# One decoder step on one core: the forget gate's chain at unit 9, its softplus at unit 7, and decode scores at unit 16

## What is computed

```python
h = h + 0.5 * post1(SwiGLU1(pre1(h)))            # 1024 -> 2816 -> 1024
P = preM(h) @ w_in                               # one combined input projection
y = [A | B | C | D](P)                           # four mixers, 256 wide each
h = h + postM(y @ w_out)
h = h + 0.5 * post2(SwiGLU2(pre2(h)))
```

```python
log_a = log_sigmoid(a_lr @ w_a2 + b_a) / 16      # B: the GLA gate
logf  = log_sigmoid(pd[..., 768:772] + b_f)      # D: the forget gate, 4 heads
s     = q k^T / 8 + cumsum(logf)_q - cumsum(logf)_k   # D: prompt scores
```

## Time and profile before

| | before |
|---|---|
| median of 3 runs | 1093.97 us (1093.46 to 1093.98) |
| the profiled execution | 1094.53 us |
| its span, first to last instruction | 1092.7 us |
| mean granted TensorE clock | 0.993 |
| busy, share of the span | PE 97%, DVE 65%, ACT 50%, POOL 25% |
| mixer stage of layer 0 / layer 1 | 211 to 325 us / 748 to 862 us |

### The profile page before, as it was taken

How to read it: one execution, slowest core, us unless ns; L and a number is a source line. 1 busy time by engine, 2 the same in 40 slices (tenths; PEclk the granted TensorE clock), 3 DMA queues, 4 the chain that set the end, 5 groups by cost and what they waited for, 6 DMA issues and landing times. The chain is left out here.

```text
span 1092.7 us, 24133 instructions
## 1 busy us (share of the span) xinstructions
PE 1064.1 (97%) x8956; PEld 1028.8 (94%) x8956; DVE 705.6 (65%) x1045; ACT 550.6 (50%) x887; POOL 274.5 (25%) x340
## 2 busy tenths in 40 slices
PE   6999999989999999999999999999899999999997
PEld 5999999988879999999999999998888899999997
DVE  5666644589995766654476665436999776666443
ACT  6544454554357644454474445446534675444542
POOL 3222221304504322220132223012053042222200
PEclk9999999999999999999999999999999999999999
DMA  7666677342726566656646666763426257656561
GB/s 269 207 186 180 179 222 232 98 155 79 232 78 196 155 193 180 184 166 187 188 127 203 180 180 188 232 186 117 139 79 209 79 190 217 180 179 176 178 181 53
DMA packets 63747, 186.92 MB, mean 171 GB/s; under 512 B 9515, under 2 KB 19763, under 8 KB 63539
## 3 DMA queue, kind: packets, MB, share of 16 engines
q1 hardware_dynamic: 63666, 185.81, 56.2%
HBM read 182.40 MB, written 3.38 MB: 170 GB/s over the span
## 5 line engine op out<-in xcount | busy, mean ns | idle before, releaser
L313 DVE TENSOR_TENSOR w_lo<-raw,w_hi 128x1024 fp32r<-128x1024 f32 (+1 forms) x316 | 411.1, 1306 | 332.0 <-ACT w_hi L303 331.8
L303 ACT ACTIVATE w_hi<-raw 128x1024 fp32r<-128x1024 f32 x336 | 342.9, 1026 | 283.0 <-PE ub L345 188.4
L343 PE MATMUL ub<-hg_hi,w_hi 128*128 128x264 f32 x960 | 278.7, 290 | 6.3 <-DVE proj L1315 6.3
L344 PE MATMUL ub<-hg_lo,w_hi 128*128 128x264 f32 x960 | 274.9, 286 | 0.0
L345 PE MATMUL ub<-hg_hi,w_lo 128*128 128x264 f32 x960 | 274.6, 286 | 0.0
L343 PE MATMUL ub<-act_hi,w_hi 128*128 128x264 f32 x704 | 200.5, 285 | 0.0
L345 PE MATMUL ub<-act_hi,w_lo 128*128 128x264 f32 x704 | 200.0, 284 | 0.0
L344 PE MATMUL ub<-act_lo,w_hi 128*128 128x264 f32 x704 | 199.1, 283 | 0.0
L343 PE MATMUL quad<-hg_hi,w_hi 128*128 128x264 f32 x688 | 196.4, 285 | 0.0
L344 PE MATMUL quad<-hg_lo,w_hi 128*128 128x264 f32 x688 | 194.9, 283 | 0.0
L345 PE MATMUL quad<-hg_hi,w_lo 128*128 128x264 f32 x688 | 194.8, 283 | 0.0
(11 more groups left out here) (252 smaller groups left out, 1314.4 us busy)
## 6 DMA issues: line engine op xcount, KB each, us to landing
raw<-in_w_gu SPq DMA_DIRECT2D x176, 512.0 KB, 4.1
raw<-in_w_dn SPq DMA_DIRECT2D x64, 512.0 KB, 4.1
raw<-in_w_in SPq DMA_DIRECT2D x44, 512.0 KB, 3.8
raw<-in_w_dn SPq DMA_DIRECT2D x32, 384.0 KB, 3.7
raw<-in_w_out SPq DMA_DIRECT2D x16, 512.0 KB, 3.7
pages<-in_cache_k SPq DMA_DIRECT2D x32, 128.0 KB, 3.3
pages<-in_cache_v SPq DMA_DIRECT2D x32, 128.0 KB, 3.1
con<-in_con SPq DMA_DIRECT2D x1, 1448.0 KB
```

The source lines that it names most:

```text
L303: eng.activation(w_hi[:, slot, 0:w], raw[:, slot, 0:w], ACT.Copy).then_inc(*sig("hi_ready", reps))
L313: eng.tensor_tensor(w_lo[:, slot, 0:w], raw[:, slot, 0:w], w_hi[:, slot, 0:w].bitcast(F32), ALU.subtract)\
L343: eng.matmul(out, a_hi, x_hi[:, k0 + k, :], start=(first and k == 0), stop=False)
L344: eng.matmul(out, a_hi, x_lo[:, k0 + k, :], start=False, stop=False)
```

## The change

Four moves; no instruction is added or removed. On ACT the forget gate's softplus goes from turn 2 to turn 7, and q's scaling from turn 4 to turn 3, so that it runs before the GLA gate's softplus instead of behind it. On DVE the forget gate's chain (lines 1067, 1069, 1123, 1125) goes from turn 3 to turn 9, ahead of that turn's mask and keys. On PE the decode scores go from turn 15 to turn 16; `gla_outputs` stays in turn 15 and is now first there. SP's program is as it was.

```diff
@@ PE, mix
                 if n == 15:
+                    gla_outputs(l)
+                if n == 16:
                     decode_scores(l, 0)
                     decode_scores(l, 1)
-                    gla_outputs(l)
                 if n == 17:
@@ ACT, mix
                     softplus(l, soft[:, :], mb[2][:, 0:NT], par[:, PAR["ba"]:PAR["ba"] + 1], "b_sp")
-                if n == 2:
+                if n == 7:
                     after(l, proj=2)
                     softplus(l, lft[:, :], proj[0:H, FG, :], par[0:H, PAR["bf"]:PAR["bf"] + 1], "d_sp")
-                if n == 4:
+                if n == 3:
                     after(l, proj=3)
                     act.activation(proj[:, BQ, :], proj[:, BQ, :], ACT.Copy, scale=DK ** -0.5).then_inc(*sig("b_qs"))
@@ DVE, mix
-                if n == 3:
+                if n == 9:
                     after(l, d_sp=3, proj=2)
                     log_sigmoid(l, lf[:, :], proj[0:H, FG, :], par[0:H, PAR["bf"]:PAR["bf"] + 1], lft[:, :], "d_lf")
```

## The result

| | before | after |
|---|---|---|
| median of 4 runs | 1093.97 us (1093.46 to 1095.72) | 1111.66 us (1109.02 to 1113.44) |
| the profiled execution | 1094.53 us | 1109.02 us |
| its span | 1092.7 us | 1107.2 us |
| mean granted clock in it | 0.993 | 0.988 |

The ratio of after to before is 1.0155, 95% interval 1.0141 to 1.0169: the change makes the kernel 1.6% slower. The forecast was 1109.4 us, between 1103 and 1116. The profiled execution is the fastest of the four after; its span is 14.5 us longer.

What follows compares the result with a forecast made beforehand. PE sets the mixer stage's time, so its start times count. Terms summed to +7.4 us in layer 0 and +8.05 in layer 1, together +15.45, taking the median from 1093.97 to 1109.4 us; range 1103 to 1116.

Steps and rivals of the forecast that it cites:

- Terms 1 to 3: PE up to unit 15: shorter wait and full clock at unit 6, +0.7 us before level 4; -2.55 us per layer.
- Term 1: PE before unit 6: the GLA gate starts earlier, the wait falls from 3.17 to about 1.7 us; -1.75 us per layer.
- Term 2: PE's unit 6: the shorter wait ahead no longer brings the clock down; -1.50 us per layer, bounds 0 and -1.50.
- Rival C: Early mixer: the short wait still lowers the clock, DVE's turn 9 holds PE longer; +2.5 per layer, 1114.4 us, chance 0.11.
- Term 4: PE before gla_norm: waits for ACT's squares, queued behind SP's later release; +9.0 us in layer 0, +9.65 in layer 1.
- Rivals A: SP's queue: issues overlap the landing, so the wait is only 1.8 us; -0.8 us per layer, 1092.4 us, chance 0.02.
- B: Before gla_norm: SP's release is not what it waits for; -2.55 us per layer, 1088.9 us, chance 0.04.
- D: Behind the long wait: units 18 to 23 all run at the low clock, 12 us per layer; about 1131 us, chance 0.03.
- Term 5: PE behind the long wait before gla_norm: the clock falls again; +1.50 us per layer, between 0 and 3.
- Rival E: Kinder clock: no price behind the long wait, unit 16 at full clock; -3.0 us per layer, 1103.4 us, chance 0.12.
- Term 6: PE's unit 16: the low clock behind gla_outputs' small matmuls stays; 0, bounds -1.5 and 0 us per layer.
- Term 7: PE before line 613: part of its 1.1 us wait goes, as PE is late; -0.55 us per layer, bounds 0 and -1.1.

Runs made afterwards that it cites:

- the late pages: The changed kernel with SP's value pages issued in turns 18 to 22 instead of two in each of turns 15 to 22; 1090.04 us, ratio 0.9958 to before.
- `lfn`: The changed kernel with only the eight lfn loads put in SP's turn 15, ahead of the value pages and the wait; 1108.13 us, ratio 1.0118 to before.
- the gates alone: The changed kernel with the decode scores put back into PE's turn 15 ahead of gla_outputs, gates moved as in the change; 1093.34 us, ratio 0.9976 to before.

## Why the prediction was right

**What bounds the kernel.** That PE's start times decide held: the seven terms leave 0.1 us per layer unexplained.

**Terms 1 to 3** are within 0.1 us in the profile. Term 1 came from adding up ACT's and DVE's durations in their new order, and ACT did wait for q's evacuation as worked out. What I did not see is that this wait was a loss of its own: I took the new order of ACT as given and asked only when its chain would end. Term 2, the clock at unit 6, I took as certain in the sum; it held in 10 of 12 layers with a wait of 1.8 us, so its mean is nearer -1.3 us. Rival C, that nothing would be gained early, is ruled out by the two layers of this profile.

**Term 4** was right in its mechanism and its size: 8.9 and 9.0 against 9.0 and 9.65. That it lies in SP's order is shown by the late pages, which take it away, and by `lfn`, a part of it. Layer 1 came out 0.7 us below its forecast for two reasons. I had taken the 13.18 us of before for the way from the release to the squares; it was 12.71, since in before the issues ahead of weight unit 20 had taken 0.5 us longer. And I had used layer 0's 3.05 us from unit 17 to `gla_norm`; in layer 1 of before it was already 3.31, since the squares ended there only 0.15 us ahead of `gla_norm`. I also called the 7.22 us SP's issues. In the trace after, the thirteen DMA instructions ahead of unit 20 take 4.3 of the 7.21 us; the rest is SP loading page numbers into registers, and small gaps. The sum does not change by that. The 0.1 us for the semaphore, which no row gave, measured 0.14. Rivals A and B are out, and D too: unit 19 took 3.01 us in both layers.

**Term 5** was too small: 2.3 and 2.8 us instead of 1.5. I priced it with the wait of 3.17 us, behind which only unit 6 paid. Behind 8.6 to 9.0 us of idling `gla_norm` ran low as well (0.75 us more) and unit 18 nearly to its end. Rival E, no price at all, is out.

**Term 6** I left at 0 with a bound of -1.5 us; it was -1.44 in layer 0 and +0.14 in layer 1 of this profile. Over all traces unit 16 is low nearly always, so 0 was the right value, and the profiled execution a lucky one. That may be why the median, 1111.66, lies 2.6 us above the profiled execution; the other three runs have no trace, and their mean clocks are 0.985, 0.986 and 0.988.

**Term 7** came out at -0.54 and -0.56 against -0.55, which I had set as the middle of its bounds.

So the profiled execution came out 1.0 us below its forecast, 1110.0, and the median 2.3 us above its own. The term that was mis-sized is term 5, by 2.1 us over both layers. In the profiled execution that was hidden: term 6 took back 1.3 us, term 4 0.8, and the shorter first stage another 0.8. That the total is so close there is in part luck. The mechanism is not luck: each wait stands in the trace where the prediction put it.

## What to carry to other kernels

When work that a DMA queue waits for is moved later, count everything that stands behind that wait in the queue's program order, not only the transfer that needs it: here pages that nobody was in a hurry for held back weights and, through ACT's own order, a step of the critical engine. Put a wait in a queue behind the transfers that don't need it. And when a step is moved ahead of another on an engine, ask for its input too: an operand that comes late makes an early place a stall.

## What the runs showed of the hardware

- The low clock does not need an idle TensorE. Unit 16 met the 1.2 GHz level in 24 of 26 layers behind 4.9 us of small matmuls (64 columns and fewer) with no recorded wait. Unit 19 did in 8 of 26 layers, behind the fox scores' matmuls of 128 and 256 columns, again with no wait recorded, and in two profiles unit 20 did as well.
- A wait of 1.81 us lowered the clock in 2 of 12 cases, one of 3.17 us in 4 of 4. The same program differs from run to run: 1084.9 to 1095.8 us in ten runs of one kernel, with mean clocks of 0.999 to 0.987. A change worth a few tenths of a per cent shows here only in PE's start times, or at equal mean clock if the waits are the same.
- "TensorE: Matmul & The Clock Gate" in the Trainium skill, section "What's actually happening", says that activity releases the throttle. The changed kernel agrees with it: behind the long waits the granted clock is back at 1.00 5.0 and 6.0 us after PE resumes. What these traces add is that PE can be busy and still run low: in the gates alone it is 0.50 over all of unit 19 in layer 0, with PE busy throughout.
- In SP's queue a page whose number comes from the page table costs more than its DMA instruction: the instruction takes 0.33 to 0.38 us, but the next page of the pair follows 1.10 us after it, because SP first loads that page's number into a register and works out the address. One of the eight tiny `lfn` loads costs 0.34 us. In this way four pages, one weight unit and eight `lfn` loads fill the 7.21 us ahead of weight unit 20, twice what that unit's 512 KB take from issue to rounding (3.58 us).
